# First products of the second and third feed-forward block in seven products of blocks (Strassen's method) for 36 of 44 pairs of feature tiles

## What is computed

```
def swiglu_ffn(h, w_in, w_out):
    a, b = jnp.split(h @ w_in, 2, axis=-1)
    return (jax.nn.silu(a) * b) @ w_out

x = x + 0.5 * swiglu_ffn(rmsnorm(x, ffn1_norm_g), ffn1_w_in, ffn1_w_out)     # f = 0
x = x + 0.5 * swiglu_ffn(rmsnorm(x, ffn2_norm_g), ffn2_w_in, ffn2_w_out)     # f = 1
x = x + (silu(h @ w_gate) * (h @ w_up)) @ w_down,  h = rms(x) * norm_ffn_w   # f = 2
```

## Time and profile before

| | us |
|---|---|
| median of 3 executions | 2400.62 (2399.74 to 2400.64) |
| the profiled execution | 2400.35 |
| its span, first to last instruction | 2398.5 |
| outside the span (start and end) | 1.85 |
| mean granted clock of TensorE | 0.998 of 2.4 GHz |

### The profile page before, as it was taken

One profiled execution on the slowest core, in us unless ns is written; L12 is line 12 of the kernel. 1 busy time (PEld: TensorE's weight loads), 2 busy tenths in 40 slices (PEclk: granted clock), 3 DMA queues, 4 the chain that ended last, 5 costly groups with the idle time before them and its releaser, 6 DMA issues.

```text
span 2398.5 us, 30453 instructions
## 1 busy us (share of the span) xinstructions
PE 2373.6 (99%) x11604; PEld 1990.7 (83%) x11604; DVE 1409.2 (59%) x2873; ACT 1000.2 (42%) x1852; POOL 182.3 (8%) x242
## 2 busy tenths in 40 slices
PE   9999999999999999999999999999999999999998
PEld 7888889888888888878888888888888887888887
DVE  6435546675757887875434446677744567543444
ACT  4223334432235676663322334666522346322332
POOL 0000000110001322210000000222100002000000
PEclk9999999999999999999999999999999999999999
DMA  4454434332322211122333234211123332323222
GB/s 149 117 121 136 117 117 141 113 99 88 114 93 84 80 54 62 55 87 97 97 92 106 97 106 123 71 62 53 62 82 112 126 111 71 95 85 110 98 85 91
DMA packets 86379, 231.31 MB, mean 96 GB/s; under 512 B 8489, under 2 KB 23465, under 8 KB 86235
## 3 DMA queue, kind: packets, MB, share of 16 engines
q1 hardware_dynamic: 81072, 221.42, 29.1%
q10 hardware_dynamic: 5162, 7.95, 2.1%
...
## 4 chain that ended last, share of the span: by engine, by line
PE 94%; DVE 4%; ACT 1%; issue 1%; POOL 0%; DMA 0%; DVEq 0%; SPq 0%; ACTq 0%
PE bank L1132 91%; PE bank L1353 2%; PE bank L1198 0%; DVE t_PS L2081 0%; DVE t_pp L2334 0%; DVE t_wlo L2076 0%; ACT t_whi L1644 0%; PE bank L1525 0%; POOL t_pw L2731 0%; DVE t_OC L2559 0%; DMA t_raw<-in_f_in 0%; DVE t_KS L2463 0%; ACT t_tmp L1644 0%; DVE t_pw L2334 0%; DVE t_XT L2698 0%
## 5 line engine op out<-in xcount | busy, mean ns | idle before, releaser
L1132 PE MATMUL bank<-t_XH,t_whi 128*128 128x512 f32 x2064 | 811.6, 393 | 2.2 <-DVE t_wlo L2123 0.9
L1132 PE MATMUL bank<-t_XH,t_wlo 128*128 128x512 f32 x2064 | 804.0, 390 | 0.0
L1132 PE MATMUL bank<-t_XL,t_whi 128*128 128x512 f32 x2064 | 803.5, 389 | 0.0
L2076 DVE TENSOR_TENSOR t_wlo<-t_raw,t_whi 128x1024 fp32r<-128x1024 f32 (+2 forms) x418 | 479.4, 1148 | 396.3 <-ACT t_whi L1644 392.7
L1644 ACT ACTIVATE t_whi<-t_raw 128x1024 fp32r<-128x1024 f32 (+3 forms) x422 | 416.8, 989 | 439.9 <-PE bank L1132 376.2
L1132 PEld LDWEIGHTS bank<-t_XH,t_whi 128*128 128x128 f32 x2064 | 387.7, 188 | 83.3 <-issue 1.8
L1132 PEld LDWEIGHTS bank<-t_XH,t_wlo 128*128 128x128 f32 x2064 | 387.4, 188 | 81.7
L1132 PEld LDWEIGHTS bank<-t_XL,t_whi 128*128 128x128 f32 x2064 | 387.9, 188 | 77.3
L1132 PE MATMUL bank<-t_RX,t_whi 128*128 128x512 f32 x1056 | 325.0, 389 | 0.0
L2193 DVE TENSOR_TENSOR t_tmp<-bank,t_RB 128x512 f32<-128x512 f32 x178 | 122.5, 688 | 199.7 <-PE bank L1132 194.4
L1132 PEld LDWEIGHTS bank<-t_RX,t_whi 128*128 128x128 f32 x1056 | 198.2, 188 | 41.0
...
## 6 DMA issues: line engine op xcount, KB each, us to landing
t_raw<-in_f_in SPq DMA_DIRECT2D x86, 512.0 KB, 3.6
...
t_raw<-in_w_conv SPq DMA_DIRECT2D x24, 512.0 KB, 3.6
t_raw<-in_w_merge SPq DMA_DIRECT2D x24, 512.0 KB, 3.6
t_raw<-in_fg SPq DMA_DIRECT2D x22, 512.0 KB, 3.6
t_raw<-in_fu SPq DMA_DIRECT2D x22, 512.0 KB, 3.6
...
t_raw<-in_w_g SPq DMA_DIRECT2D x16, 512.0 KB, 3.6
```

The costliest lines, as they stand in the source:

```text
L1132: return e.matmul(o, l, r, start=start, stop=stop, skip_group_check=True)
L2076: e.tensor_tensor(wlo[n % NRAW][:, 0:width], raw[n % NRAW][:, 0:width], f32(whi[n % NHI][:, 0:width]), ALU.subtract).then_inc(*w_lo.tick(n))
```

## The change

With [A | B] the two weight units of a pair and x cut into two halves of its features and two halves of its positions, a and b of a pair are a 2 x 2 product of blocks: (2 x 128 outputs) x (2 x 512 features) times (2 x 512 features) x (2 x 256 positions). The new code makes it from seven products of blocks instead of eight, in Winograd's form, in which four sums of weight blocks, four sums of x blocks and seven sums of results are made:

- Pairs 3 to 10 of half 0 and 1 to 10 of half 1 in blocks 1 and 2 (`SEVEN`, `PLAIN`) are 4 x 9 = 36 pairs. The other 8 pairs of these blocks and all of block 0 stay.
- `prod` (TensorE): one of seven products, 4 x 3 = 12 matmuls of 128 x 256 each, in the order 1, 5, 2, 6, 4, 3, 7, into four banks; 6, 3 and 7 go on top of what an earlier product left in its bank. Products 1, 2 and 4 use weight blocks as loaded, 5, 6, 7 and 3 the sums.
- `wsum` (POOL, four per pair): a sum or difference of two 128 x 512 parts of the raw units, into SR. The first, third and fourth wait for the pair's second unit to land, all but the first for its first unit.
- `wcut` (ACT and DVE, four per pair): high and low parts: 0 is the whole first unit (its low part overwrites raw, so it waits for the last `wsum`), 1 half of the second, 2 and 3 the sums, 1024 columns each.
- `keep` (ACT, four per pair): copies a bank's 256 columns. `join` (DVE, four per pair): adds a bank and such a copy. `rate` (POOL, two per pair): the 128 x 512 multiply by RB. `silu` (ACT), `gate` (DVE), `hidden` (ACT and DVE) as in `ffg` before.
- `mix` (POOL, 16 sums of 128 x 256 per block) and `mixed` (ACT, DVE): the sums of x blocks, made beside the plain pairs 1 and 2 of half 0. ACT first writes the scaled x into SR (8 copies per block).
- The work of a pair's weights (`wsum`, `wcut`) is placed a pair ahead, the results (`join` 7 and 8, `rate` 1, `gate`, `hidden`) run a pair behind. Stages 2 and 7 get an order in `TIMES`. In these lists four to six POOL instructions stand from a pair's first `wsum` to its fourth, in the 32 cases where a pair is prepared beside another seven-product pair: 163 in all, 5.1 in the mean.
- `winload` is issued in half 1 of block 1 instead of half 0; the wait for x moves from `norm` to `normsq` where there is no gain.

```diff
+SEVEN = (1, 2)
+PLAIN = (3, 1)
+HX = S // 2
...
+        def register(key):
+            if key not in w.seven:
+                j = key[1] * KF + key[2]
+                w.seven[key] = (w.unit(wa, oa + j), w.unit(wb, ob + j), len(w.seven))
+
+        def prepare(key):
+            register(key)
+            for i in range(4):
+                w.add("wsum", *key, i)
+                w.add("wcut", *key, i)
+
+        def seven(h):
+            keys = [(f, h, m) for m in range(PLAIN[h], KF)]
+            for before, key, after in zip([None, *keys], keys, [*keys[1:], None]):
+                w.both = 0
+                register(key)
+                if after:
+                    register(after)
+                w.both = 2 if after else 1
+
+                def ahead(kind, i):
+                    if after:
+                        w.add(kind, *after, i)
+
+                def behind(*items):
+                    if before:
+                        for kind, *i in items:
+                            w.add(kind, *before, *i)
+
+                w.add("prod", *key, 1)
+                behind(("join", 7), ("join", 8), ("rate", 1))
+                ahead("wsum", 0)
+                w.add("prod", *key, 5)
+                w.add("keep", *key, 1)
+                ahead("wsum", 1)
+                w.add("prod", *key, 2)
+                w.add("keep", *key, 5)
+                ahead("wcut", 1)
+                ahead("wsum", 2)
+                behind(("gate",))
+                w.add("prod", *key, 6)
+                w.add("join", *key, 2)
+                ahead("wsum", 3)
+                behind(("hidden",))
+                w.add("prod", *key, 4)
+                w.add("keep", *key, 6)
+                ahead("wcut", 0)
+                w.both = 2 if after else 0
+                w.add("prod", *key, 3)
+                w.add("keep", *key, 4)
+                ahead("wcut", 2)
+                w.add("prod", *key, 7)
+                w.add("join", *key, 3)
+                w.add("rate", *key, 0)
+                ahead("wcut", 3)
+                w.add("silu", *key)
+            w.both = 0
+            for kind, *i in (("join", 7), ("join", 8), ("rate", 1), ("gate",), ("hidden",)):
+                w.add(kind, *keys[-1], *i)
+
...
+    SR = [place(f"SR{q}", 2048 * q, 2048) for q in range(2)]
+    SL = [place(f"SL{q}", 2048 * q, 2048, F32R) for q in range(2)]
+    SH = [place(f"SH{q}", (4096, 17920)[q], 2048, F32R) for q in range(2)]
+    TXH, TXL = (place(f"TX{q}", 19968 + 4096 * q, 4096, F32R).rearrange("p (k i n) -> p k i n", k=4, i=4) for q in range(2))
+    P1T, U2T, P5T = (place(f"part{q}", 28160 + HX * q, HX) for q in range(3))
...
+    FIRST = {1: "ra", 5: "rc", 2: "rb", 4: "rd"}
+    THEN = {6: "ra", 3: "rc", 7: "ra"}
+    BLOCK = {1: 0, 2: 1, 4: 2}
+    SUM = {5: 0, 6: 1, 7: 2, 3: 3}
+    MIX = {5: 0, 6: 1, 7: 2, 4: 3}
...
+    def pair_tiles(m):
+        return T[2 * m % 4], T[2 * m % 4 + 1]
+
...
+        def prod(f, h, m, q):
+            n, n2, j = w.seven[f, h, m]
+            key, ni = (f, h, m), (0, 2, 5)[f]
+            b = take("d", (FIRST[q], *key)) if q in FIRST else banks[(THEN[q], *key)]
+            if q == 6:
+                on.wait_ge(*copied.at(("p1", *key)))
+            if q == 3:
+                on.wait_ge(*copied.at(("p5", *key)))
+            if q == 7:
+                on.wait_ge(*copied.at(("u2", *key)))
+            if q in BLOCK:
+                unit, c0 = ((n, n2)[BLOCK[q] > 1], (0, 512)[BLOCK[q] > 0])
+                hi, lo = weights(unit)
+                done = ("u", unit) if q != 1 else ("a11", n)
+            else:
+                i = SUM[q]
+                on.wait_ge(*w_hi.at(("s", j, i // 2)))
+                on.wait_ge(*w_lo.at(("s", j, i // 2)))
+                hi, lo, c0, done = SH[j % 2], SL[j % 2], 512 * i, ("us", j, i)
+            for k in range(4):
+                if q in (1, 2, 3):
+                    kx, t = k + 4 * (q > 1), slice(HX * (q == 3), HX * (q == 3) + HX)
+                    operand(("n", ni, kx))
+                    xh, xl = XH[:, kx, t], XL[:, kx, t]
+                else:
+                    operand(("tx", f, k))
+                    xh, xl = (x[:, k, MIX[q], :] for x in (TXH, TXL))
+                c = slice(c0 + k * P, c0 + (k + 1) * P)
+                last = three(b[:, 0:HX], hi[:, c], lo[:, c], xh, xl, q in FIRST and k == 0, k == 3)
+            last.then_inc(*full.tick(("prod", *key, q), done))
...
+        def wcut(f, h, m, i):
+            n, n2, j = w.seven[f, h, m]
+            if i < 2:
+                u, c = (n, n2)[i], slice(512 * i, 1024)
+                on.wait_ge(*d_raw[u % NRAW].at(u))
+                on.wait_ge(*full.at(("u", u - NHI)))
+                copy(whi[u % NHI][:, c], raw[u % NRAW][:, c]).then_inc(*w_hi.tick(u))
+            else:
+                c = slice(1024 * (i - 2), 1024 * (i - 1))
+                on.wait_ge(*summed.at(("sum", j, 2 * i - 3)))
+                for q in (2 * i - 4, 2 * i - 3):
+                    on.wait_ge(*full.at(("us", j - 2, q)))
+                copy(SH[j % 2][:, c], SR[j % 2][:, c]).then_inc(*w_hi.tick(("s", j, i - 2)))
+
+        def keep(f, h, m, q):
+            key = (f, h, m)
+            before = pair_before(key)
+            on.wait_ge(*full.at(("prod", *key, q)))
+            if q == 4:
+                if m >= 2:
+                    on.wait_ge(*x_hi.at(("g", f, h, m - 2)))
+                    on.wait_ge(*x_lo.at(("g", f, h, m - 2)))
+                copy(pair_tiles(m)[1][:, 0:HX], banks[("rd", *key)][:, 0:HX]).then_inc(
+                    *copied.tick(("c4", *key), ("free", ("rd", *key))))
+                return
+            o, name, reader = {1: (P1T, "p1", "c11"), 5: (P5T, "p5", "c22"), 6: (U2T, "u2", "c12")}[q]
+            if before:
+                on.wait_ge(*evac.at((reader, *before)))
+            copy(o, banks[("rc" if q == 5 else "ra", *key)][:, 0:HX]).then_inc(*copied.tick((name, *key)))
+
+        def silu(f, h, m):
+            a = pair_tiles(m)[0]
+            on.wait_ge(*summed.at(("a", f, h, m)))
+            e.activation(a, a, ACT.Silu).then_inc(*curve.tick(("silu", f, h, m)))
+
+        def hidden(f, h, m):
+            on.wait_ge(*calc.at(("ffg", f, h, m)))
+            copy(GH[:, m, :], pair_tiles(m)[1]).then_inc(*x_hi.tick(("g", f, h, m)))
...
+        def wcut(f, h, m, i):
+            n, n2, j = w.seven[f, h, m]
+            if i < 2:
+                u, c = (n, n2)[i], slice(512 * i, 1024)
+                on.wait_ge(*w_hi.at(u))
+                on.wait_ge(*summed.at(("sum", j, 0 if i else 3)))
+                e.tensor_tensor(wlo[u % NRAW][:, c], raw[u % NRAW][:, c], f32(whi[u % NHI][:, c]), ALU.subtract).then_inc(*w_lo.tick(u))
+            else:
+                c = slice(1024 * (i - 2), 1024 * (i - 1))
+                on.wait_ge(*w_hi.at(("s", j, i - 2)))
+                on.wait_ge(*summed.at(("sum", j, 3)))
+                e.tensor_tensor(SL[j % 2][:, c], SR[j % 2][:, c], f32(SH[j % 2][:, c]), ALU.subtract).then_inc(
+                    *w_lo.tick(("s", j, i - 2)))
+
+        def join(f, h, m, q):
+            key = (f, h, m)
+            a, b = pair_tiles(m)
+            if q in (2, 7) and m >= 2:
+                on.wait_ge(*x_hi.at(("g", f, h, m - 2)))
+                on.wait_ge(*x_lo.at(("g", f, h, m - 2)))
+            name, other, o, done, more = {
+                2: ("rb", P1T, a[:, 0:HX], "c11", [("free", ("rb", *key))]),
+                3: ("rc", U2T, a[:, HX:S], "c12", [("free", ("rc", *key))]),
+                7: ("ra", P5T, b[:, HX:S], "c22", []),
+                8: ("ra", b[:, 0:HX], b[:, 0:HX], "c21", [("free", ("ra", *key))])}[q]
+            on.wait_ge(*full.at(("prod", *key, min(q, 7))))
+            on.wait_ge(*copied.at(({2: "p1", 3: "u2", 7: "p5", 8: "c4"}[q], *key)))
+            e.tensor_tensor(o, banks[(name, *key)][:, 0:HX], other, ALU.add).then_inc(*evac.tick((done, *key), *more))
+
+        def gate(f, h, m):
+            a, b = pair_tiles(m)
+            on.wait_ge(*summed.at(("b", f, h, m)))
+            on.wait_ge(*curve.at(("silu", f, h, m)))
+            e.tensor_tensor(b, b, a, ALU.mult).then_inc(*calc.tick(("ffg", f, h, m)))
...
+        def wsum(f, h, m, i):
+            n, n2, j = w.seven[f, h, m]
+            a, b = raw[n % NRAW], raw[n2 % NRAW]
+            s = [SR[j % 2][:, 512 * q:512 * q + 512] for q in range(4)]
+            x, y, op = ((b[:, 0:512], b[:, 512:1024], ALU.add), (s[0], a[:, 0:512], ALU.subtract),
+                        (a[:, 0:512], b[:, 0:512], ALU.subtract), (a[:, 512:1024], s[1], ALU.subtract))[i]
+            if i != 1:
+                on.wait_ge(*d_raw[n2 % NRAW].at(n2))
+            if i:
+                on.wait_ge(*d_raw[n % NRAW].at(n))
+            if i in (1, 3):
+                on.wait_ge(*summed.at(("sum", j, i - 1 if i == 1 else 1)))
+            if j >= 2:
+                on.wait_ge(*full.at(("us", j - 2, i)))
+            if (f, h, m) in OPENING:
```

(51 more changed lines are left out.)

102 lines of the change are left out of this document (91 added, 11 removed).

## The result

The change makes the kernel slower: 2484.96 us (2482.88 to 2488.59) against 2400.18 for the kernel before on the same chip, a ratio of 1.0357 with a 95% interval of 1.0345 to 1.037. That is +85 us where +14 was forecast and where 2437 was the end of the range.

A forecast was written before the change was run, and what follows sets the result against it. TensorE bounds the kernel before; after the change, DVE and POOL taking turns and the weights' chain bound a pair. +17.0 and -3.2 give +13.8 on 2400.35, 2414 us; own range 2401 to 2437, whole range 2374 to 2437.

The forecast's parts named there:

- 32 pairs beside a preparation: Seven-product pairs run while a next one is prepared: 11.4 us each instead of 10.87, +17.0 us in all.
- 4 last pairs: Last pair of each of the four half blocks, with nothing to prepare: 0.79 us less each, -3.2 us in all.
- the two starts: Sums made beside plain pairs at the start of blocks 1 and 2: costed at nothing, 0 to 5 us per block.
- The paces of TensorE: Matmul steps: 0.2264 us for 512 columns, 0.1200 for 256; a seven-product pair 10.08 us against 10.87, 0.79 less.
- DVE and POOL together: Their two-input SBUF instructions take turns, 10.55 to 11.7 us a pair, over TensorE's 10.08; joins don't count.
- the starved rival: DVE instructions in a row keep POOL out altogether: 13.4 us a pair, +77 us, 2477 us; chance 0.12.
- The pair's price: A seven-product pair takes 11.4 us, in the upper part of the turns' range; TensorE waits 1.3 us in each.
- the sum of turns: Per pair, DVE's 5.75 us plus six POOL instructions at 0.80 to 0.99 each: 10.55 to 11.7 us.
- The 12.1: Time in us of the weights' chain for pair 9, half 0, block 1: load, six POOL instructions, `gate`, `wcut` 0, hold-ups.
- The discount for shorter chains: Where four or five POOL instructions stand in the chain with `gate` behind, it is 1.3 to 2.6 us less.
- The clock: TensorE's granted clock, 1.00 before; its fall in stretches with waits would prove the prediction wrong; no cost given.
- ACT's `keep`: TensorE waits before products 6, 3 or 7 for a bank copy stuck behind a `wcut`: +10 us, 2410; chance 0.05.

The follow-up runs named there:

- the plain order: The change without the written-out orders of stages 2 and 7, so each engine follows the order of the program: 2551.06 us.
- the runs with fills: The change with POOL's weight sums and multiplies by RB as fills that read nothing: two each 2394.11 us, one 2385.35, one also for x sums 2381.74.
- the fillers: The change with 6 needless 128x256 matmuls ahead of the wait before products 1 and 5 of each pair: 2480.22 us.

## Why the prediction was wrong

The span grew by 88.3 us where the sum had 13.8. By its terms:

| | forecast | measured |
|---|---|---|
| 32 pairs beside a preparation | 32 x (11.4 - 10.87) = +17.0 | 32 x (12.88 - 10.87) = +64.3 |
| 4 last pairs | 4 x -0.79 = -3.2 | +5.3 (12.2 us each) |
| the two starts | 0 (0 to 5 per block) | 8.0 + 10.3 = +18.3 |

- *The paces of TensorE* (0.2264 and 0.1200 us, 0.79 a pair) held. Steps between waits are 0.120, and where nothing was late, stretches shrank by 3.9 us for five pairs.
- *DVE and POOL together* was the right mechanism, and its signs held: subtractions of 1024 at 1618 ns, sums at 1440 to 1634 (near 1.8 us was forecast), and 91 us less without POOL's reads, at least 55 of them, by the estimate above, for the reads alone. The Trainium skill's rule (SBUF — State Buffer, Who interferes with whom), that the second fully blocks, was cited for the starved rival; the time, 2485, is close to that rival's 2477, which had 0.12. But POOL did not starve: its mean of 1.6 us is less than half a subtraction over 1.27, and it is idle for a third of the stretches. The rival had nearly the right time by the wrong count.
- *The pair's price*, 11.4 us, is the step that failed, 47 of the 74 us of error. It was taken from the sum of turns, a bound from below, with turns that are hardly ever idle. The prediction had also worked out 12.1 for a chain that goes through one pair after the other and had set it aside as that of the worst pairs. The pace is that of such a chain: 12.9 us in the mean, and 12.92 in the loop of the plain order. The 12.1 was itself short. Each POOL instruction is held up by 0.39 us on average in the pair above (9.94 us for six), 2.3 us in all where 1.36 was put in; and the multiplies by RB wait for joins (1.5 us there), since they stand between the sums.
- *The discount for shorter chains* failed too. Pairs with four or five POOL instructions from first to last `wsum` were to be 1.3 to 2.6 us shorter. By the trace it is 12.6 us for those with four (9 pairs), 13.2 with five (11) and 12.7 with six (12). That count does not sort the pairs; the loop holds all six instructions of a pair wherever they stand.
- *The last pairs* were to run at TensorE's pace because they prepare nothing. The longest, 14.0 us, waits 2.2 us for a join; it and the one of 12.8 us, whose own first cut was 2.9 us late, then have 17 and 27 steps at half clock. This is 8.5 us of the error. In the runs with fills they take 10.1 to 10.4.
- *The starts* cost 18.3 us where nothing was put into the sum. ACT, POOL and DVE being half idle says nothing of a chain in order: x sums wait for scaled copies, the first weight sums stand behind 16 x sums on POOL, and cuts wait behind both. In block 2 the norm's `t_rn` is late as well.
- *The clock* was named only as something that would prove the prediction wrong. It fell, to 0.92 to 0.95. Its 25 us of slow steps lie within the pairs' 12.9 us; by the fillers 5 to 7 us of them come back at the least.
- *ACT's `keep`* held TensorE up once, for 1.4 us. Joins did for 13.1 us in the four stretches, which the prediction did not list.
